# End of the decay attention: gate pieces before the last level, squares in halves, second norm with tokens on partitions

## What is computed

```python
def rms_norm(x, g):
    xf = x.astype(jnp.float32)
    return (xf * lax.rsqrt(jnp.mean(xf * xf, axis=-1, keepdims=True) + RMS_EPS)).astype(x.dtype) * g

def hgrn2(q_raw, f_fwd_raw, f_bwd_raw, i_raw, g_raw, lb, norm_g):
    ...
    o = direction(f_fwd_raw, lb[0], False) + direction(f_bwd_raw, lb[1], True)
    o = rms_norm(o, norm_g) * jax.nn.silu(heads(g_raw))
    return o.astype(g_raw.dtype)

def even_mixer(h, w_in, w_out, diff_lambda, subln_g, lb, hg_norm_g, cos, sin, lam_init):
    ...
    oa = rms_norm(diff_attention(qa, ka, va, lam), subln_g) * (1.0 - lam_init)
    ob = hgrn2(qb, f_fwd, f_bwd, ib, gb, lb, hg_norm_g)
    o = jnp.concatenate([oa.reshape(B, L, DIFF_WIDTH).astype(h.dtype), ob.reshape(B, L, HG_WIDTH)], axis=-1)
    return o @ w_out
```

## Time and profile before

| | |
|---|---|
| three runs | 2828.92, 2833.66, 2839.65 us |
| profiled execution, its span | 2832.9 us |
| mean granted clock of PE | 0.975 of full speed |
| PE, DVE, ACT busy | 2685.2, 1905.3, 1095.6 us |
| share of the chain that ended last: PE, DVE, ACT, DMA | 82%, 12%, 2%, 2% |

### The profile page before, as it was taken

How to read it: one execution, slowest core, us unless ns; L and a number is a source line. 1 busy time by engine, 2 the same in 40 slices (tenths; PEclk the granted TensorE clock), 3 DMA queues, 4 the chain that set the end, 5 groups by cost and what they waited for, 6 DMA issues and landing times.

```text
span 2832.9 us, 44344 instructions
## 1 busy us (share of the span) xinstructions
PE 2685.2 (95%) x17806; PEld 2160.0 (76%) x17806; DVE 1905.3 (67%) x1945; ACT 1095.6 (39%) x875; POOL 111.8 (4%) x154
## 2 busy tenths in 40 slices
PE   6989999977899999999999987899999999999998
PEld 2348888833588888888888861688888888888887
DVE  6876666678556676776777769676776666555555
ACT  4463333354433333334444431144433333444442
POOL 1011000000001100000000011000020000000000
PEclk9999999998999999999999998999999999999999
DMA  8888878822352887887878849478657777555551
GB/s 244 335 318 291 285 260 283 268 67 83 120 163 99 279 285 254 285 289 259 283 267 286 279 162 220 158 243 283 233 170 238 237 233 236 176 192 178 189 184 57
DMA packets 245071, 635.19 MB, mean 224 GB/s; under 512 B 33154, under 2 KB 34820, under 8 KB 240356
## 3 DMA queue, kind: packets, MB, share of 16 engines
q1 hardware_dynamic: 232260, 579.27, 61.1%
q0 software_dynamic: 9536, 34.48, 4.1%
q10 hardware_dynamic: 3168, 19.92, 1.8%
HBM read 613.83 MB, written 19.79 MB: 224 GB/s over the span
## 4 chain that ended last, share of the span: by engine, by line
PE 82%; DVE 12%; ACT 2%; DMA 2%; issue 1%; SPq 0%; DVEq 0%; ACTq 0%
PE PS L271 46%; PE PS L275 23%; PE PS L224 3%; DVE Pb L1883 2%; DVE acc L1878 1%; PE PS L960 1%; PE PS L763 1%; DMA araw<-in_ada_w 1%; PE PS L188 1%; PE PS L740 1%; PE PS L926 1%; DVE wlo L261 1%; PE PS L469 1%; PE PS L673 1%; DVE X L1502 1%
## 5 line engine op out<-in xcount | busy, mean ns | idle before, releaser
L271 PE MATMUL PS<-H,whi 128*128 128x512 f32 x5888 | 1863.9, 397 | 21.5 <-DVE wlo L261 13.8
L261 DVE TENSOR_TENSOR wlo<-raw,whi 128x2048 fp32r<-128x2048 f32 x368 | 844.1, 2294 | 698.4 <-ACT whi L257 697.3
L275 PEld LDWEIGHTS PS<-H,wlo 128*128 128x128 f32 x5888 | 1112.2, 189 | 262.2
L257 ACT ACTIVATE whi<-raw 128x2048 fp32r<-128x2048 f32 x368 | 705.6, 1918 | 1228.6 <-PE PS L271 1207.4
L275 PE MATMUL PS<-H,wlo 128*128 128x256 f32 x5888 | 1161.6, 279 | 0.0
L271 PEld LDWEIGHTS PS<-H,whi 128*128 128x128 f32 x5888 | 903.5, 190 | 27.5 <-DVE wlo L261 21.0
L180 DVE SCALAR_TENSOR_TENSOR acc<-araw,cact,acc 128x1024 f32<-128x1024 f32 x240 | 307.9, 1283 | 2.0 <-DMA araw<-in_ada_w 1.5
L1035 ACT ACTIVATE Pb<-PS 128x1024 f32 (+5 forms) x109 | 107.9, 1003 | 119.2 <-PE PS L673 52.5
L1035 ACT ACTIVATE H<-Pb 128x512 fp32r (+3 forms) x138 | 90.6, 657 | 32.9 <-DVE Pb L1494 22.5
L1556 DVE TENSOR_TENSOR H<-Pb,H 128x512 fp32r<-128x512 f32 x128 | 87.7, 685 | 0.0
L1994 POOL TENSOR_SCALAR X<-X,small 128x256 f32<-128x256 f32 x64 | 64.9, 1028 | 484.0 <-DVE Pb L1494 469.4
(11 more groups left out here) (274 smaller groups left out, 1406.4 us busy)
## 6 DMA issues: line engine op xcount, KB each, us to landing
raw<-in_mlp_w SPq DMA_DIRECT2D x256, 1024.0 KB, 6.0
araw<-in_ada_w SPq DMA_DIRECT2D x274, 512.0 KB, 4.5
raw<-in_mix_w_in SPq DMA_DIRECT2D x64, 1024.0 KB, 7.5
raw<-in_s_w_glu SPq DMA_DIRECT2D x32, 1024.0 KB, 7.3
acc<-in_ada_w SPq DMA_DIRECT2D x40, 512.0 KB, 8.0
raw<-in_ada_w POOLq DMA_DIRECT2D x32, 512.0 KB, 4.1
raw<-in_mix_w_out SPq DMA_DIRECT2D x16, 1024.0 KB, 5.2
vmat<-Pb ACTq DMA_DIRECT2D x8, 1024.0 KB, 7.2
```

The lines of the kernel that those rows point to most:

```text
L257: nc.scalar.activation(whi[:, s % 2, :], raw[:, s, :], ACT.Copy).then_inc(S("hi_done"), 1)
L261: nc.vector.tensor_tensor(wlo[:, s % 2, :], raw[:, s, :], whi[:, s % 2, :].bitcast(F), ALU.subtract).then_inc(S("lo_done"), 1)
L271: return nc.tensor.matmul(PS[:, b, :], w, H2[:, :, k, :], start=first, stop=last, skip_group_check=True)
L275: return nc.tensor.matmul(PS[:, b, 0:T], w, H2[:, 0, k, :], start=False, stop=last, skip_group_check=True)
```

## The change

- `GATE_SPLIT` becomes `(16, 18, 21, 24, 27, 30, 32, 32)`: three pieces behind levels 1 to 4, two behind level 5, none behind level 6. `gate_turn` moves behind level 7's products. Level 7 no longer has the gate ahead of it.
- SP loads the output product's first four slabs outside its loop: two when `gate_used` is 32, two more when `level_arg(7)` has read `LN_KEY`. ACT and DVE split slabs 0 and 1 before the norm instead of after it.
- The score-value products signal after four heads and after eight. ACT squares each half straight from PSUM into `SQ` (the copy to `OB` is gone); DVE multiplies each half in PSUM by `GH`, which already carries the norm's weight.
- The norm's sums are taken with the squares as weights and one column of ones as the moving side (`rms_tokens_pe`): 16 products of one column each, whose result has tokens on partitions, 128 x 16. Root and reciprocal work on 128 x 16, and 16 products of 128 x 128 with the identity spread it again into banks 0 to 3, half by half. Root's table is loaded early by a one-column instruction.
- `Hhi` and `Hlo` of the first attention are made between the halves, those of the second in halves.
- Of the 43 idle products around this norm two are left, between the sums and the spreading.
- The output product uses banks 4 to 7 first (`swap`), and the layer norm behind it takes banks 5 and 6.
- Some semaphores of the setup and of layer 1 are joined (`consts`, `prepared`, `ld_lay`), with the same waits at the same places.

```diff
-    GATE_SPLIT = (16, 18, 20, 22, 24, 26, 29, 32)
+    GATE_SPLIT = (16, 18, 21, 24, 27, 30, 32, 32)
...
+    def rms_tokens_pe(pe):
+
+        for half in range(2):
+            pe.wait_ge(S("rms_sq"), 2 + half)
+            for z in range(8 * half, 8 * half + 8):
+                last = nc.tensor.matmul(PS[:, 0, z:z + 1], SQ[:, z * P:(z + 1) * P], ones[:, 0:1],
+                                        start=True, stop=True)
+        last.then_inc(S("rms_sum"), 1)
+        idle_products(2, 3)
+        pe.wait_ge(S("rms_inv"), 2)
+        for half in range(2):
+            for z in range(8 * half, 8 * half + 8):
+                last = nc.tensor.matmul(PS[:, z // 4, (z % 4) * P:(z % 4 + 1) * P],
+                                        RSTD2[:, z:z + 1].broadcast_to([P, P]), ident[:], start=True, stop=True)
+            last.then_inc(S("rms_wide"), 1)
...
             sp.wait_ge(S("gate_used"), 32)
-            for s in plan_out:
-                stream(s)
+            slab_loads(sp, 0, s.B, s.G, s.src, slabs=range(2))
+            sp.wait_ge(S("lv_arg"), 14)
+            slab_loads(sp, 0, s.B, s.G, s.src, slabs=range(2, 4))
+            with sp.Fori(1, s.bodies) as i:
+                slab_loads(sp, i, s.B, s.G, s.src)
...
-                    if lv == 6:
+                    if lv == 7:
                         pe.wait_ge(S(f"{SCALE1.name}_freed"), 1)
                         gate_turn(pe)
                 pe.wait_ge(S("sc_ready"), 4)
                 pe.wait_ge(S("lv_put"), 7)
                 for h in range(8):
+                    if h == 4:
+                        last.then_inc(S("hg_pv"), 1)
+                        pe.wait_ge(S("gate_out"), 1)
...
                 act.wait_ge(S("gate_used"), 32)
                 run(GATE_TURN, PS[0:GATE_ROWS, 6, :], sem="turn_copied")
+                run(STD2[:, 0:1], eps[:, 1:2], ACT.Sqrt)
+                act.wait_ge(S("lv_mm"), 9)
+                run(SCO[:, 0].rearrange("p h t -> p (h t)"), bank(2, 2), sem="sc_ready")
                 act.wait_ge(S("turn_T"), 2)
                 run(SHIFT_SUM, PS[:, 7, 0:16], sem="gate_out")
-                act.wait_ge(S("lv_mm"), 9)
-                run(SCO[:, 0].rearrange("p h t -> p (h t)"), bank(2, 2), sem="sc_ready")
-                act.wait_ge(S("hg_pv"), 1)
-                link(run(OB, bank(4, 4)))
-                rms_square(2, OB)
-                rms_root(2)
-                act.wait_ge(S("o_ready"), 1)
-                run(Hhi[:, 0:8, :], Pb[:, 0:8, :], sem="o_hi")
-                run(Hhi[:, 8:16, :], Pb[:, 32:40, :], sem="o_hi")
+                for sl in range(2):
+                    split_hi(act, 0, plan_out[0].B, plan_out[0].G, sl)
+                for half in range(2):
+                    act.wait_ge(S("hg_pv"), 1 + half)
+                    run(SQ[:, 1024 * half:1024 * half + 1024], bank(4 + 2 * half, 2), ACT.Square, "rms_sq")
+                    if half == 0:
+                        act.wait_ge(S("oa_final"), 1)
+                        run(Hhi[:, 0:8, :], Pb[:, 0:8, :], sem="o_hi")
+                act.wait_ge(S("rms_sum"), 2)
+                link(run(STD2, PS[:, 0, 0:16], ACT.Sqrt, scale=1.0 / P, bias=eps[:, 1:2]))
...
+            link(ts(GH, GH, HGG, None, ALU.mult))
+            split_lo(v, 0, plan_out[0].B, plan_out[0].G, 0)
...
+            gated_out(0)
+            split_lo(v, 0, plan_out[0].B, plan_out[0].G, 1)
+            gated_out(1)
+            v.wait_ge(S("o_hi"), 1)
+            oa_low(0)
+            v.wait_ge(S("rms_std"), 2)
+            link(nc.vector.reciprocal(RSTD2, STD2))
+            v.sem_inc(S("rms_inv"), 1)
+            oa_low(1)
```

More of the change, by code:

```diff
@@ L275, in low, with wide_products @@
         return nc.tensor.matmul(PS[:, b, 0:T], w, H2[:, 0, k, :], start=False, stop=last, skip_group_check=True)
-    def wide_products(pe, evacs, slabs, par, h=None, sums=None, before=None, freed=None):
+    def wide_products(pe, evacs, slabs, side, h=None, sums=None, before=None, freed=None):
         pe.wait_ge(S("evac_done"), evacs)
@@ L291, in wide_products @@
                 for kt in (0, 2):
[L292 to L295, removed]
+                    high(4 * side + m, whi[:, s % 2, at[kt]], 4 * s + kt, first=(s == 0 and kt == 0))
+                    low(4 * side + m, wlo[:, s % 2, at[kt]], 4 * s + kt, last=False)
+                    low(4 * side + m, wlo[:, s % 2, at[kt + 1]], 4 * s + kt + 1, last=False)
+                    last = high(4 * side + m, whi[:, s % 2, at[kt + 1]], 4 * s + kt + 1, first=False,
                                 last=(s == 3 and kt == 2))
@@ L580, in _ @@
                             o = 64 * g + 16 * r
-                            load(IM[o:o + 16], lags[g][:, :, 48 - 16 * r:112 - 16 * r], "ld_im")
+                            load(IM[o:o + 16], lags[g][:, :, 48 - 16 * r:112 - 16 * r], "ld_lay")
                     for n in range(12, 16):
@@ L677, in _, with run_block @@
             gemv_turn(pe)
[L679 removed]
+            def run_block(s, h=None, swap=0):
                 def body(i, par, first=False, freed=None):
[L682 removed]
+                    wide_products(pe, i * 2 + (s.E + par + 1), i * 8 + (s.G + 4 * par + 1 + PRIME_RAW), par ^ swap,
                                   None if par else h, s.sums if first else None, s.E + PRIME_EVAC, freed)
@@ L1002, in _ @@
             for s in plan_out:
-                run_block(s, 1)
+                run_block(s, 1, swap=1)
             layer_norm_pe(0)
@@ L1163, in layer_norm_act @@
                 act.wait_ge(S("ln_psum"), 2 * k + 2)
-                run(LNS, PS[:, LN_BANK[k % 2] + 1, 0:T], ACT.Sqrt, "ln_std", scale=1.0 / D, bias=eps[:, 0:1])
-            def rms_square(n, o):
-                run(SQ[n - 1], o, ACT.Square, "rms_sq")
-            def rms_root(n):
-                act.wait_ge(S("rms_sum"), n)
-                run(RS[n - 1], PS[0:ROWS, 0, 0:T], ACT.Sqrt, "rms_std", scale=1.0 / P, bias=eps[0:ROWS, 1:2])
+                run(LNS, PS[:, LN_BANK[k] + 1, 0:T], ACT.Sqrt, "ln_std", scale=1.0 / D, bias=eps[:, 0:1])
             def attention_act():
@@ L1207, in attention_act @@
                             run(LN_KEY[d], (FF_, FB_)[d], ACT.Ln, "hg_ln", bias=TINY)
-                rms_square(1, OA)
+                run(SQ, OA, ACT.Square, "rms_sq")
             def hgrn_act():
@@ L1226, in hgrn_act @@
                     if lv == 0:
-                        rms_root(1)
+                        act.wait_ge(S("rms_sum"), 1)
+                        run(RS, PS[0:ROWS, 0, 0:T], ACT.Sqrt, "rms_std", scale=1.0 / P, bias=eps[0:ROWS, 1:2])
                     if lv == 6:
@@ L1298, in _ @@
             for s in plan_out:
-                with act.Fori(0, s.bodies) as i:
+                for sl in range(2, 4):
+                    split_hi(act, 0, s.B, s.G, sl)
+                with act.Fori(1, s.bodies) as i:
                     for sl in range(4):
@@ L1790, in _ @@
             level_arg(1)
-            rms_inverse(1)
+            v.wait_ge(S("rms_std"), 1)
+            link(nc.vector.reciprocal(RS, RS))
+            v.sem_inc(S("rms_inv"), 1)
             level_mul(0)
```

110 lines of the change are left out of this document (57 added, 53 removed).

## The result

Four runs of each kernel: 2803.56 us median with the change (2800.53 to 2805.03), 2831.29 us before. The ratio is 0.9902, 95% interval 0.9887 to 0.9918: 27.7 us faster, between 23 and 32. I had forecast 24.1 us, 2809.6 us, with 2803 to 2818 us as range. The profiled execution has a span of 2802.2 us, 30.7 us under that of before.

What follows compares the result with a forecast made beforehand. The prediction took a latency chain across ACT, PE and DVE before the output product as the bound. 26.0 us earlier less 1.9 us for the clock gave 24.1 us, 2809.6 us as median, range 2803 to 2818 us.

Steps and rivals of the forecast that it cites:

- The place: Chain from level 7 to the output product: its earlier start carries the whole gain, 24.1 us.
- Level 7, 6.0 us: Level 7's products (L867 before) follow the queries without gate pieces and transposes ahead: start 6.0 us earlier.
- the sign that L883 starts within 0.3 us of DVE's last query product: Check at level 7: its products L883 start within 0.3 us of DVE's last query product, right behind L874.
- Pieces at levels 1 to 4, cost 0: Gate pieces moved to earlier levels fit into PE's waits: cost 0, without this cover up to 2 us.
- Sums, root, spreading: Second norm: sums about 3.7 us, root 0.18 and reciprocal 0.2 us hidden by two idle products (1.0 us), spreading 3.6 us.
- Second attention: Output product's third slab: second attention ready near 766 us, needed at 773.7 us, 7 us of cover.
- The clock, 1.9 us: Lower clock behind the one-column sums, at spreading and output product: loss between 0 and 3.4 us, taken as 1.9 us.
- 26.0 us as the gain at the full clock: Output product starts at 762.5 instead of 788.48 us, 26.0 us earlier, before any clock loss.
- Root's table, no drain: Early table load on ACT ahead of level 7's end: cost 0; with a drain of 1.38 us the gain would be 22.8 us.
- the third rival: Whole kernel: more gain than summed, no clock loss and shorter hand-offs, 2802 to 2806.7 us; chance 0.07.
- that of the first: First rival, whole kernel: as summed, gain 22 to 27 us, 2806.7 to 2811.7 us; chance 0.62.
- R's edits: Rival of the follow-up runs: banks and joined semaphores elsewhere give 4 to 7 us of the gain; no chance stated.

Runs made afterwards that it cites:

- the rest alone: Kernel before with only the output product's bank swap, the layer norm's new banks and the joined semaphores: 2832.44 us, ratio 1.0008.
- pieces alone: Kernel before with only the new `GATE_SPLIT` and the gate's transposes moved behind level 7's products: 2825.86 us, ratio 0.9987.
- pieces back: Changed kernel with the gate pieces back at their old levels (`GATE_SPLIT` of before), all else as changed: 2807.14 us, ratio 0.9919.
- old form: Changed kernel with the second norm's old form: sums with heads on partitions, root and reciprocal on 12 x 256: 2810.21 us, ratio 0.9923.

## Why the prediction was right, point by point

**The place.** The gain came where forecast: 24.2 and 24.7 us between level 6 and the output product in two profiles, against 24.1 us. Runs that undo one part each lose about what its term says, and more where the lower clock follows; those that remove idle products alone or the rest alone gain nothing. The four parts undone one by one (pieces, form of the norm, early splits, halves) come to 18.9 us; the remainder was not undone by itself.

**Level 7, 6.0 us.** In the second profile of the changed kernel level 7 starts 2.4 us behind level 6, before it was 8.4 us: 6.0 us. In the first it is 4.8 us, since level 6 itself ran at the lower clock. So the sign that L883 starts within 0.3 us of DVE's last query product held in the second (742.08, then 742.19 us) and not in the first (742.14, then 743.43 us).

**Pieces at levels 1 to 4, cost 0.** Held for PE's work: level 6 waits 3.91 us for DVE in the first profile and 2.42 us in the second, more than the 2.21 us of before. The forecast had seen only that PE would not be late. It had missed the other side: in the first profile levels 6 and 7 lost 2.5 us at the lower clock, a cost that the sum had at nothing. The fourteen profiles point to that rest, without proving it: level 6 was slow in the two with the longest one ahead of it, 3.9 us (this one and pieces alone), and took 2.1 us in the other twelve.

**Sums, root, spreading.** From the start of the score-value products to the end of the sums I had 10.9 us; it is 10.8 us (749.64 to 756.86 + 3.63 = 760.49). To the spreading 1.0 us forecast, 0.8 us measured. Spreading 3.6 us forecast, 3.78 us measured at the full clock. The root took 0.27 us, not 0.18 us, the reciprocal 0.25 us: hidden by the two idle products. Second attention ready long before the third slab: held.

**The clock, 1.9 us.** Taking 26.0 us as the gain at the full clock, 1.8 us and 1.3 us were lost in the two profiles. The size was right, the mechanism only in one: the sum had put the lower clock behind the one-column sums, where it came in the second profile, but in the first the window behind them reads 1.00 and the loss was at levels 6 and 7. That it was 1.8 us there as well is luck. Nor do one column and the lower clock belong together, as the runs with sums of 256 columns show. The forecast also called 1.47 us PE's one longer pause; the one ahead of level 6, 2.21 us in the earlier trace rows, was longer. Here the rule of the Trainium skill weighed in the prediction ("TensorE: Matmul & The Clock Gate", Part 1), that the throttled state is the default and activity releases it, agrees with the fall at levels 6 and 7, behind a rest of PE of 3.91 us, and with the 14.0 us of rest in the kernel of before without its tail. In the second profile the clock fell behind the one-column sums although PE had not paused since the score-value products began.

**Root's table, no drain.** Held: the one-column root starts 0.02 us behind the load's end (746.22 + 1.28, 747.52). The drain of some 1.38 us that the Trainium skill gives in "ScalarE: Activation LUTs" (What ACT_TABLE_LOAD costs) is not there in these rows.

**The size of the whole.** 27.7 us measured against 24.1 us, an interval of 23 to 32 us. The time is only 0.6 us inside the stated range, and it lies in the span of the third rival (2802 to 2806.7 us). The traces do not show that rival's mechanism, no clock loss and shorter hand-offs: up to the output product the gain was that of the first. The number came out lower because of what lies behind that start, for which the forecast had no term, and that it stayed within the range is in part luck.

In both profiles the span shrank by 6.6 to 7.1 us more than the start of the output product moved. About 3 us of this is the one execution of before that was profiled: nearly every recorded run lies 1.7 to 2.0 us above its own span, so the span of 2832.9 us belongs to a run of some 2834.7 us, 3.4 us above the median of before. From the start of the output product to the end the four profiles of before and the kernels built on it need 2044.4, 2041.8, 2040.4 and 2040.2 us, the ten of the changed kernel and those built on it 2033 to 2046 us, 2038.4 us in the mean. So the difference is about 3 us and the spread within one family four times that.

The engines do the same work there, and much of the spread goes with the clock. The granted clock's distance from 1.00 times the length, summed over 200 windows of that stretch, is 27.6 us in the shortest (pieces back, 2033.2 us) and 43.5 us in the longest (old form, 2045.7 us). It is 42.7 us in before, 35.6 to 36.1 us in the other three of its family, and 38.5 and 33.6 us in the two profiles of the changed kernel. R's edits can give at most 1.4 us of the difference. Whether an earlier start shifts the lower clock for the better, or ten and four executions merely fell so, stays open; by the intervals the whole measured gain can be that of the chain.

## What to carry to other kernels

Idle products that keep a clock up also hide how long a chain is: look for what else ends at the same moment. Here removing them alone moved the start by 0.5 us and the time not at all, and once the chain had shrunk by 24 us the same products cost 13 us. A busy PE is to be asked which of its products anybody reads.

Work that is moved out of a wait into another has two effects, and both want a row: the wait that it fills, and the new rest where it was. Give a reduction the layout that makes the small steps behind it narrow: 128 x 16 instead of 12 x 256 took the reciprocal from 1.74 us to 0.25 us with the same time on PE.

## What was unexpected of the hardware

- The same kernel had its lower clock at levels 6 and 7 in one execution and behind the sums in the next, at nearly the same total (25.0 and 24.5 us).
- With sums of 64 columns instead of one the 32 records took the same time (3.68 and 3.63 us); in both the 32 weight loads took 3.65 us, so these may set the pace.
- Products behind a rest can stay slow: after 14.0 us without work the first L271 took 0.80 us instead of 0.58 us, and the first 4.4 us of the output product ran at 0.54.
